# A hybrid diffusion step on one core: more projection products in the first nine mixer steps, and GpSimd's spreads between the low parts of the weights

## What is computed

```python
def trunk_layer(x, cond, lw, na_fn, s0_f, s0_b, rope):
    mods = (silu(cond) @ lw['w_ada'] + lw['b_ada'])[:, None, :]
    shift1, scale1, gate1, shift2, scale2, gate2 = split(mods, 6)
    h = rms_norm(x, lw['norm1_gain']) * (1 + scale1) + shift1
    u_pool, q_na, k_na, v_na, q_la, k_la, v_la, g_la, lr_f, lr_b = split(h @ lw['w_in'])
    y_pool = pool_mixer(u_pool, ...)             # A: centred means, windows 2, 4, 8, 16
    q_na, k_na = rms_norm(q_na), rms_norm(k_na)  # per head of 64
    y_na = na_fn(q_na, k_na, v_na)               # B: neighbourhood attention, 8 heads
    y_la = gla_mixer(q_la, k_la, v_la, g_la, lr_f, lr_b, ...)  # C: gated linear attention, chunks of 64, both ways
    x = x + gate1 * (concatenate([y_pool, y_na, y_la]) @ lw['w_out'])
    h2 = rms_norm(x, lw['norm2_gain']) * (1 + scale2) + shift2
    return x + gate2 * swiglu(h2, lw['w_ffn_in'], lw['w_ffn_out'])
```

## Time and profile before

| | us |
|---|---|
| median of 3 runs | 1757.54 |
| lowest and highest | 1757.44, 1759.84 |
| the profiled execution | 1757.72 |
| its span in the trace | 1755.9 |

### The profile page before, as it was taken

How to read it: one execution, slowest core, us unless ns; L and a number is a source line. 1 busy time by engine, 2 the same in 40 slices (tenths; PEclk the granted TensorE clock), 3 DMA queues, 4 the chain that set the end, 5 groups by cost and what they waited for, 6 DMA issues and landing times. The chain is left out here.

```text
span 1755.9 us, 29168 instructions
## 1 busy us (share of the span) xinstructions
PE 1678.0 (96%) x12024; PEld 1610.0 (92%) x12024; DVE 1038.4 (59%) x1885; ACT 558.6 (32%) x910; POOL 585.4 (33%) x281
## 2 busy tenths in 40 slices
PE   5979999999999999999999789998999999999998
PEld 4878889889999999999998678897999999999998
DVE  3477455758887488528777855566677713331342
ACT  4322455343322122112343225444332212221221
POOL 1135111126333334333452421111544333333332
PEclk9889899999999999999999989998999999999999
DMA  9234312112443344334331011210233222222223
GB/s 366 73 130 157 104 63 72 53 37 96 137 150 125 127 144 143 97 96 150 110 118 61 15 40 67 67 67 25 81 102 117 96 72 72 74 81 74 72 63 105
DMA packets 51306, 171.01 MB, mean 97 GB/s; under 512 B 6352, under 2 KB 9232, under 8 KB 51088
## 3 DMA queue, kind: packets, MB, share of 16 engines
q1 hardware_dynamic: 51216, 169.81, 29.5%
HBM read 165.98 MB, written 3.80 MB: 97 GB/s over the span
## 5 line engine op out<-in xcount | busy, mean ns | idle before, releaser
L536 POOL TENSOR_TENSOR w_lo<-w_raw,w_hi 128x1024 fp32r<-128x1024 f32 (+2 forms) x196 | 499.6, 2550 | 1083.9 <-ACT w_hi L637 1050.2
L637 ACT ACTIVATE w_hi<-w_raw 128x1024 fp32r<-128x1024 f32 (+2 forms) x194 | 200.3, 1033 | 674.2 <-PE acc L1367 609.9
L1367 PE MATMUL acc<-h_lo,w_hi 128*128 128x320 f32 (+1 forms) x1456 | 335.3, 312 | 0.0
L1367 PE MATMUL acc<-h_hi,w_hi 128*128 128x320 f32 (+1 forms) x1456 | 335.2, 312 | 0.0
L1367 PEld LDWEIGHTS acc<-h_hi,w_hi 128*128 128x128 f32 x1456 | 246.6, 190 | 1.6 <-issue 1.3
L1367 PEld LDWEIGHTS acc<-h_lo,w_hi 128*128 128x128 f32 x1456 | 246.3, 189 | 0.0
L1367 PE MATMUL acc<-h_hi,w_lo 128*128 128x320 f32 (+1 forms) x1456 | 230.3, 310 | 0.0
L1367 PEld LDWEIGHTS acc<-h_hi,w_lo 128*128 128x128 f32 x1456 | 219.7, 189 | 0.0
L1225 DVE SCALAR_TENSOR_TENSOR x<-acc,mods,x 128x320 f32<-128x320 f32 (+2 forms) x192 | 72.6, 434 | 221.9 <-PE acc L1367 200.9
L1367 PE MATMUL acc<-y_lo,w_hi 128*128 128x320 f32 x808 | 183.9, 309 | 0.0
L1367 PE MATMUL acc<-y_hi,w_hi 128*128 128x320 f32 x808 | 183.9, 309 | 0.0
(11 more groups left out here) (245 smaller groups left out, 2200.1 us busy)
## 6 DMA issues: line engine op xcount, KB each, us to landing
w_raw<-in_w SPq DMA_DIRECT2D x176, 512.0 KB, 3.5
mod_w<-in_w_ada SPq DMA_DIRECT2D x56, 512.0 KB, 4.5
w_gm<-in_w_ada SPq DMA_DIRECT2D x24, 512.0 KB, 4.6
bias<-in_bias SPq DMA_DIRECT2D x16, 576.0 KB, 4.6
w_ada<-in_w_ada SPq DMA_DIRECT2D x16, 512.0 KB, 13.6
w_raw<-in_w SPq DMA_DIRECT2D x16, 384.0 KB, 3.1
x<-in_x SPq DMA_DIRECT2D x4, 640.0 KB, 9.4
out_x<-x SPq DMA_DIRECT2D x8, 320.0 KB, 3.9
```

The lines of the kernel that those rows point to most:

```text
L536: pool.tensor_tensor(w_lo[p][:, 0:n], raw[p][:, 0:n], w_hi[p][:, 0:n].bitcast(F32), ALU.subtract).then_inc(lo_made[p], 1)
L637: act.activation(w_hi[p][:, 0:n], raw[p][:, 0:n], ACT.Copy).then_inc(hi_made[p], 1)
L1367: mm = pe.matmul(acc[p][:, half, 0:m.shape[-1]], w[:, k * P:(k + 1) * P], m, start=w is w_hi[p] and k == 0 and part is hi, stop=w is w_lo[ ...
```

## The change

The first 15 steps get their own shares of products, `EARLY_PRODUCTS`; from step 16 or 17 on the count is as before, since the larger of both is taken. In products done before each step:

| step | 1 | 2 | 3 | 4 | 5 | 6 | 7 | 8 | 9 | 10 | 12 | 14 | 16 | 17 |
|---|---|---|---|---|---|---|---|---|---|---|---|---|---|---|
| before | 14 | 28 | 43 | 57 | 72 | 86 | 100 | 115 | 129 | 144 | 172 | 201 | 230 | 244 |
| now | 16 | 32 | 56 | 82 | 108 | 134 | 154 | 174 | 192 | 200 | 216 | 230 | 236 | 244 |

Tiles 0 to 3 are finished in steps 2, 4, 6 and 8 (before 3, 6, 9 and 13). The evacuation, shift and next high part of each move with it. GpSimd's spreads stand in other places between the low parts. The load of the cached keys and values, with that of the bias, stands behind one tile more in SP's queue, and so do the loads of the last four gate pairs. ScalarE waits once more, before it overwrites the squares' buffer.

```diff
@@ product_at @@
+EARLY_PRODUCTS = (16, 16, 24, 26, 26, 26, 20, 20, 18, 8, 8, 8, 8, 6, 6)
+
+
 def product_at(step):
 
     if step <= HEAD_STEPS * PAIRS:
-        return step * 3 * MMS // HEAD_STEPS
+        return max(sum(EARLY_PRODUCTS[:step]), step * 3 * MMS // HEAD_STEPS)
@@ sync @@
-                    if t == (T_K if l else T_PAIR + 4):
+                    if t == (T_K if l else T_PAIR + 5):
@@ gpsimd @@
                         q_by_head(0)
                         states_by_head(0)
+                    if t == T_PAIR + 2:
                         q_by_head(1)
-                    if t == T_PAIR + 2:
-                        for j in range(1, NP):
-                            if j + 1 < NP:
-                                q_by_head(j + 1)
-                            states_by_head(j)
+                        states_by_head(1)
+                        q_by_head(2)
+                    if t == T_PAIR + 3:
+                        states_by_head(2)
+                        q_by_head(3)
+                        states_by_head(3)
+                    if t == T_PAIR + 4:
+                        q_by_head(4)
+                        states_by_head(4)
@@ scalar @@
                             row = (qn, kn)[n % 3][:, c % 2, :]
+                            if n == 0:
+                                act.wait_ge(full["O"], after("O", "kdb", l))
                             link(shifted(t, by_column(row)))
```

## The result

| | before | after |
|---|---|---|
| median | 1757.76 (4 runs, 1757.44 to 1759.84) | 1803.29 (4 runs, 1792.33 to 1803.51) |
| ratio | | 1.0241, 95% interval 1.0202 to 1.0280 |
| the profiled execution | 1757.72 | 1803.39 |
| its span | 1755.9 | 1801.6 |

The account below looks back on a forecast made before the run. It took PE's work plus idle and half-clock time as the bound. Added idle of 10.2 us in layer 1 and 11.0 in layer 0, plus 1.4 for clock, gave +22.6 on 1757.72: 1780, range 1768 to 1790.

Parts of the forecast that it names:

- What bounds the kernel: Whole kernel: PE busy 1678.0 of 1755.9 us, so without matmuls added or removed only idle and half-clock time can move.
- GpSimd's order and the waits: Steps 4 to 9: low parts of weights queued behind spreads make PE wait, 7.6, 6.4 and 5.1 us in layer 1's steps 4, 6, 8.
- s and low: GpSimd's spread of a pair's states, taken as 2.8 us, and low part of product tile n's weights, low(n), 2.65 us.
- q: GpSimd's spread of the queries for one pair, taken as 2.3 us.
- Step 4's sum of arrivals: Layer 1, step 4: PE reaches tile 2 at 973.9, its low part ends at 981.5, so PE waits 7.6 us.
- Layer 0: the waits: Steps 0 to 16 of layer 0: idle 26.2 us against 15.2 before, +11.0.
- The clock: Half clock after long waits in steps 4, 6, 8: 1.3 us each, less two old stretches; net +0.7 a layer, +1.4 together.
- The trade in steps 10 to 16: 44 products left instead of 100: 2.2 us wait in step 13 plus 0.5 in steps 14 to 16, 2.7 a layer.
- The ends of the range: 1768 with quicker GpSimd and no late waits or clock charges; 1790 with longer late waits, a late load, more half clock.
- Rival (d): Steps 5 to 9: GpSimd also holds VectorE's masks and key products, PE waits for VectorE; 1790 to 1800, chance 7%.
- the sum: Forecast total over both layers: idle +10.2 and +11.0, clock +1.4, together +22.6 us.
- Rival (a): Products fill the old waits, low parts being ready in time; 9.3 us of each layer vanish, 1739, chance 4%.

Follow-up runs that it names:

- The even tail's execution: The changed kernel with 9 products a step from step 9 to 20, where it had 8 or fewer until step 16: 1788.81, ratio 1.0183.
- the second profile of the kernel after: The changed kernel run and profiled once more, with no edit: 1796.22, ratio 1.0224.
- the filled versions: The changed kernel with GpSimd's low parts ahead of the spreads, plus unread matmuls: 10 in step 13, 1754.30; with 12 more in step 9, 1747.41.
- the early low parts: The changed kernel, same product table, with GpSimd's low parts of the weights queued ahead of the spreads they stood behind: 1756.66, ratio 1.0007.

## Why the prediction was right and wrong

**What bounds the kernel: right, and half applied.** It said that a change which keeps the matmuls can only move idle time and time at half clock. The second of the two turned out the larger.

**GpSimd's order and the waits: right.** In layer 1, forecast and measured:

| step | 4 | 6 | 7 | 8 | 9 | 10 to 16 | sum |
|---|---|---|---|---|---|---|---|
| forecast | 7.6 | 6.4 | 1.5 | 5.1 | 3.7 | 2.7 | 27.0 |
| measured | 7.81 | 5.99 | 1.52 | 4.13 | 3.06 | 2.5 | 25.0 |

The durations taken were a little high for s and low (2.8 and 2.65, measured 2.69 and 2.52) and a little low for q (2.3, measured 2.40). Step 4's sum of arrivals held to 0.2 us. Undoing the order alone took nearly the whole loss away (1.0007), which shows it as the cause.

**Layer 0: the waits were over-sized, for a reason not seen.** Forecast for steps 4, 6, 8, 9: 7.6, 5.3, 4.0, 3.0; measured 6.05, 3.57, 1.82, 3.45; sum 21.2 against 26.2. The even tail's execution, with more of the same steps at full clock, shows 7.5 for step 4, 4.98 for tile 3 and 3.16 for step 8, and the second profile of the kernel after 7.55, 5.16 and 3.16, near the forecast but for step 8: half-clock work stood in place of part of the waits.

**The clock: the step that failed.** The prediction charged 1.3 us for each of three long waits, took off two old stretches, and came to +0.7 a layer. Busy time rose by 18.5 and 8.7 us instead, 27.2 against 1.4. The 1.3 came from the first 32 scores after a wait, and even these rows give 2.55 - 1.54 = 1.0: the price was read at one group of instructions, and not over the whole stretch until the clock was back. In layer 0 after, the wait that ended at 163.66 has a half-clock stretch to 169.6, and a second one, with no wait over 0.2 us between the two, lies from 173.0 to 179.8; 6.8 us at half clock cost up to 3.4. The products there, in PE's timeline, before and after the rise:

```profile
176.31 0.74 PE L1362 MATMUL acc<-h_hi,w_hi 128*128 128x320 f32 x2
...
180.26 0.45 PE L1362 MATMUL acc<-h_hi,w_lo 128*128 128x320 f32 x2
```

The trace of before had a better price. Its windows with waits of 4.6 to 6.5 us stand at 0.76, 0.84, 0.73 and 0.75, and over both layers 15.2 + 16.8 us of idle time went with 23.9 + 17.1 at half clock: 1.3 us of half clock for each us of idle, costing up to half of itself. By that the 21.2 us of idle forecast bring 27 at half clock and up to 13.6 of busy time, and the forecast would have been about 1757.7 + 21.2 + 13.6 = 1792.5. It would still have been low, since the ratio itself rose: 105.8 us at half clock for 46.2 idle, 2.3 to one. So the ratio is a better estimate and no rule.

The Trainium skill, TensorE: Matmul & The Clock Gate, "What's actually happening", says that activity releases the throttle, which agrees with the filled versions (0.54 to 1.00 in steps 14 to 16, with 10 matmuls put in front).

**The trade in steps 10 to 16: the wait right, the clock missed.** Idle 2.5 us against 2.7 in both layers. But the windows show 0.79 and 0.71. In layer 1 steps 9 to 16 took 33.2 us against 38.0 before, with 63 x 0.148 = 9.3 us less work: 4.5 lost, though idle time there hardly changed (5.6 against 5.5).

**The ends of the range.** Upward 1.3 us a layer had been set for a longer stretch at half clock; beyond the 0.7 already charged, 12.9 a layer would have been needed. Rival (d), the nearest in time, has the wrong mechanism: after GpSimd's waits PE doesn't wait for VectorE's masks and key products. VectorE was slower beside GpSimd: this group of four took 2.27 us and, beside the spreads of step 6, 3.94, but no wait of PE ends on it. VectorE's timeline:

```profile
1017.82 2.27 DVE L1013 TENSOR_TENSOR kk<-bcum 128x256 f32<-128x256 f32 x4
...
1026.89 3.94 DVE L1013 TENSOR_TENSOR kk<-bcum 128x256 f32<-128x256 f32 x4
```

**Chance.** 4.4 of the 45.7 us are the stretch ahead of step 0. Without it 41.3 remain, still 18.7 above the sum. That gap is the difference of two larger errors, and hides part of the second: the idle time was forecast 7.0 us too long (21.2 against 14.2), the busy time 25.8 too short (1.4 against 27.2). The queues of SP and ScalarE cost nothing, as forecast: nothing outside steps 0 to 16 changed, and PE's waits for DMAs in layer 0's steps stayed at 3.6 us (3.4 before).

**Rival (a)** said that if low(2) came early the products would fill the waits and 9.3 us a layer vanish. Its condition was a wait under 3.5 us at tile 2; with the early low parts it was 3.57, and there was none at tile 3. Even so 9.3 us a layer didn't come: the clock took the gain, and with the waits of steps 9 and 13 filled it was 3.2 and 5.8.

## What to carry to other kernels

Where PE stands near its bound, count a wait at its own length plus what the granted clock takes behind it, up to the point where it is back at full speed, and take the ratio from the windows of the kernel before, as a lower estimate: here it was 1.3 before and 2.3 after. When a table moves work forward, check the engine that makes its inputs: here the place of three low parts in GpSimd's queue decided between +2.2% and nothing, measured side by side. A short wait that can't be removed can be filled with matmuls nobody reads, but only where PE truly waits.

## What was not expected of the hardware

The same matmuls on the same queue took 7.7 us more or less in layer 0's steps 0 to 8, and 5.0 us more or less in the stretch ahead of step 0, from execution to execution. There the place of the half clock mattered as much as its amount: the kernel before had 10.2 us of it and was busy for 70.05, the second profile of the kernel after 27.3 and was busy for 69.78, the first 27.3 and 74.88. Adding 44 matmuls to layer 0 made it 9 to 10 us shorter, part of it scatter, and adding them to layer 1 made that 3.4 to 3.8 us shorter. Ten of them in a wait of 2.31 us brought the 44 instructions of the three steps behind to 7.8 us, from 9.2 to 13.0. Why steps of layer 0 that have no wait stay at half clock in some executions and not in others is open.
